# Turning the probabilities of block 2's 64-wide heads by VectorE blocks and a trip through memory instead of by TensorE

## What is computed

```python
def swa_gqa_sinks(q, k, v, sinks):
    ...
    scores = jnp.einsum("bnqhgd,bnkhd->bnhgqk", qb, kw).astype(jnp.float32) * (A_HEAD_DIM ** -0.5)
    ...
    scores = jnp.where(valid[None, :, None, None], scores, -jnp.inf)
    mx = jnp.maximum(jnp.max(scores, axis=-1, keepdims=True), sink)
    pr = jnp.exp(scores - mx)
    den = jnp.sum(pr, axis=-1, keepdims=True) + jnp.exp(sink - mx)
    attn = (pr / den).astype(v.dtype)
    out = jnp.einsum("bnhgqk,bnkhd->bnqhgd", attn, vw)
```

## Time and profile before

| | |
|---|---|
| median of 3 runs | 2307.66 us (2304.9 to 2308.04) |
| profiled execution, its own time | 2307.95 us |
| its span from first to last instruction | 2306.2 us |
| TensorE's mean granted clock | 0.998 of full speed |
| TensorE busy | 2283.7 us, 99% |
| VectorE busy | 1527.7 us, 66% |
| ScalarE busy | 1233.8 us, 53% |
| DMA engines, mean share | 61.7% by the weight and scratch queue |

### The profile page before, as it was taken

One profiled execution on the slowest core, in us unless ns is written; L12 is line 12 of the kernel. 1 busy time (PEld: TensorE's weight loads), 2 busy tenths in 40 slices (PEclk: granted clock), 3 DMA queues, 4 the chain that ended last, 5 costly groups with the idle time before them and its releaser, 6 DMA issues.

```text
span 2306.2 us, 30120 instructions
## 1 busy us (share of the span) xinstructions
PE 2283.7 (99%) x11144; PEld 1906.6 (83%) x11144; DVE 1527.7 (66%) x2411; ACT 1233.8 (53%) x1890; POOL 128.6 (6%) x141
## 2 busy tenths in 40 slices
PE   9999999999999999999999999999999999999999
PEld 8887888888878888888878888888888888888887
DVE  6656786566567866576587765664766587657654
ACT  6555544445555454354467654554554478555543
POOL 3140000004300000000000000000000000000000
PEclk9999999999999999999999999999999999999999
DMA  8556568756475587577564444875677564456772
GB/s 336 199 192 238 190 220 290 228 185 214 156 267 186 172 287 242 180 256 248 189 230 157 157 155 165 265 241 195 219 244 238 178 215 156 150 171 209 233 235 89
DMA packets 179857, 483.08 MB, mean 209 GB/s; under 512 B 20480, under 2 KB 65152, under 8 KB 178688
## 3 DMA queue, kind: packets, MB, share of 16 engines
q1 hardware_dynamic: 179712, 481.16, 61.7%
HBM read 452.24 MB, written 28.84 MB: 209 GB/s over the span
## 4 chain that ended last, share of the span: by engine, by line
PE 92%; DVE 3%; DMA 3%; ACT 1%; SPq 1%; issue 1%; POOL 0%; DVEq 0%; ACTq 0%
PE bank L2104 27%; PE bank L2109 27%; PE bank L2108 27%; PE bank L2151 2%; PE bank L2091 2%; PE bank L2092 2%; PE bank L2093 2%; DMA raw<-in_weights 1%; DVE wl L1593 1%; PE bank L2240 1%; SPq L1181 1%; DMA rg<-moved 1%; DMA moved<-rv 0%; PE bank L2202 0%; PE bank L2225 0%
## 5 line engine op out<-in xcount | busy, mean ns | idle before, releaser
L1363 ACT ACTIVATE wh<-raw 128x1024 fp32r<-128x1024 f32 (+1 forms) x778 | 814.5, 1051 | 768.1 <-PE bank L2109 690.8
L1593 DVE TENSOR_TENSOR wl<-raw,wh 128x1024 fp32r<-128x1024 f32 (+1 forms) x778 | 927.8, 1223 | 282.9 <-ACT wh L1363 279.3
L2104 PE MATMUL bank<-wh,xh 128*128 128x512 f32 (+1 forms) x2102 | 826.8, 393 | 5.0 <-issue 3.9
L2109 PE MATMUL bank<-wh,xl 128*128 128x512 f32 (+1 forms) x2102 | 816.8, 389 | 0.0
L2108 PE MATMUL bank<-wl,xh 128*128 128x512 f32 (+1 forms) x2102 | 815.7, 388 | 0.0
L2104 PEld LDWEIGHTS bank<-wh,xh 128*128 128x128 f32 x2102 | 395.2, 188 | 87.0 <-issue 7.3
L2109 PEld LDWEIGHTS bank<-wh,xl 128*128 128x128 f32 x2102 | 394.9, 188 | 81.0
L2108 PEld LDWEIGHTS bank<-wl,xh 128*128 128x128 f32 x2102 | 395.5, 188 | 76.9
L2104 PE MATMUL bank<-wh,act_h 128*128 128x512 f32 x528 | 206.0, 390 | 0.0
L2109 PE MATMUL bank<-wh,act_l 128*128 128x512 f32 x512 | 199.4, 389 | 0.0
L2108 PE MATMUL bank<-wl,act_h 128*128 128x512 f32 x512 | 199.3, 389 | 0.0
(11 more groups left out here) (347 smaller groups left out, 2066.9 us busy)
## 6 DMA issues: line engine op xcount, KB each, us to landing
raw<-in_weights SPq DMA_DIRECT2D x760, 512.0 KB, 4.3
turn<-ffn_s SPq DMA_DIRECT2D x264, 64.0 KB, 2.8
ffn_a<-turn SPq DMA_DIRECT2D x66, 256.0 KB, 4.7
raw<-in_weights SPq DMA_DIRECT2D x16, 384.0 KB, 3.2
ln<-in_ln SPq DMA_DIRECT2D x4, 1024.0 KB, 6.8
moved<-merged SPq DMA_DIRECT2D x32, 128.0 KB, 3.5
merged<-moved SPq DMA_DIRECT2D x8, 512.0 KB, 7.0
bias<-in_bias SPq DMA_DIRECT2D x2, 1024.0 KB, 9.3
```

Source lines behind the costliest of these rows:

```text
L1363: act.activation(wh[:, u % NH, 0:used(u)], raw[:, u % NR, 0:used(u)], ACT.Copy).then_inc(hi_done, 1)
L1593: dve.tensor_tensor(wl[:, u % NR, 0:used(u)], raw[:, u % NR, 0:used(u)], wh[:, u % NH, 0:used(u)].bitcast(F32), ALU.subtract).then_inc(lo_ ...
L2104: pe.matmul(out, h, w_h, start=st.first and i == 0, stop=False)
L2109: last = pe.matmul(out, lo, w_h, start=False, stop=ends)
```

## The change

1. Block 2's 16 heads: the 32 `probs_T` steps (16 in each layer) are gone. Instead each pair of heads has its probabilities, 128x768, transposed in 32x32 blocks by one VectorE instruction (`block`), written to scratch by four DMAs (`out`) and read back by one (`back`) into one of three buffers; `aa_pv` then reads them from there with a pattern of runs of 32 numbers. To make the order of the pieces fit, the two parts of a head's scores change places in `Pn`.
2. The pairs no longer go through `heads` but through a table: pair p starts at `PAIRS_AT[p]`, its `even` comes 2 later, `block` 3, `out` 4, `back` 6 and `aa_pv` 8 later. The digits of `weave` become lists of places (`PLACES_1`, `PLACES_2`).
3. The transfers of `ak`, `aq0` and `aq1` are issued earlier, among the units of the chunk `aq1` and after it, and the copies of `ak` and `aq0` stand at places 2 and 3 instead of 4 and 5.
4. In block 1 the steps from the copy of `rq` on stand earlier: the retention's steps at places 18 to 22 instead of 22 to 27, `block` of `rg0` and `rg1` at 23 instead of 28, their `out` at 24 and 25 instead of 29 and 30, `back` at 27 and 28 instead of 31 and 32, `halve` at 30 and 31 instead of 33 and 34. The loads `bm12` and `ln1` (1 MB each) stand at 31, behind these, instead of at 28, ahead of them. The later attention of block 1 stands one or two places earlier.

The places of block 2's pairs, worked out from the tables (scores / even / block / out / back / product):

| pair | before: scores, even, transposes, product | after: scores, even, block, out, back, product |
|---|---|---|
| 0 | 6, 7, 10 and 11, 12 | 6, 8, 9, 10, 12, 14 |
| 1 | 8, 12, 14 and 15, 16 | 8, 10, 11, 12, 14, 16 |
| 2 | 12, 16, 17 and 18, 19 | 12, 14, 15, 16, 18, 20 |
| 3 | 16, 18, 20 and 21, 23 | 15, 17, 18, 19, 21, 23 |
| 4 | 19, 22, 24 and 25, 27 | 19, 21, 22, 23, 25, 27 |
| 5 | 23, 26, 31 and 31, 32 | 22, 24, 25, 26, 28, 30 |
| 6 | 27, 32, 34 and 35, 37 | 26, 28, 29, 30, 32, 34 |
| 7 | 32, 36, 37 and 37, 38 | 29, 31, 32, 33, 35, 37 |

```diff
+PAIRS_AT = (6, 8, 12, 15, 19, 22, 26, 29)
+PAIR_STEPS = (("pv", 8), ("even", 2), ("s", 0), ("block", 3), ("out", 4), ("back", 6))
...
     for r in range(R):
         h_a = p.moved("block", f"rg{r}", rows=p.cc["rows"], dst="oa", tile=r)
-    p.add("load", name="bm12", s=ret_s3, roped=roped)
-    p.add("load", name="ln1", roped=roped)
     for r in range(R):
         h_a = p.moved("out", f"rg{r}", rows=p.cc["rows"], dst="oa", tile=r)
+    for r in range(R):
+        h_a = p.moved("back", f"rg{r}", rows=p.cc["rows"], dst="oa", tile=r)
     for src in ("dq", "dk"):
         c_d = p.moved("block", src, roped=q[src + "_rope"].n)
     for r in range(R):
-        h_a = p.moved("back", f"rg{r}", rows=p.cc["rows"], dst="oa", tile=r)
+        h_a = p.moved("halve", f"rg{r}", rows=p.cc["rows"], dst="oa", tile=r)
+    p.add("load", name="bm12", s=ret_s3, roped=roped)
+    p.add("load", name="ln1", roped=roped)
...
-    q["o"] = heads(p, "aa", AH // 2, scores, q["akv"])
+    done, evens = {}, {}
+    for _, _, what, pair in sorted((at + after, k, what, pair) for pair, at in enumerate(PAIRS_AT)
+                                   for k, (what, after) in enumerate(PAIR_STEPS)):
+        h = 2 * pair
+        if what == "s":
+            done[h] = scores(h)[1]
+        elif what == "even":
+            evens[pair] = p.count("even", 2)
+            p.add("even", h=h, of="aa", soft=done[h], m=p.count("shares"))
+        elif what == "block":
+            p.moved("block", f"pair{pair}", h=h, m=evens[pair])
+        elif what in ("out", "back"):
+            p.moved(what, f"pair{pair}", h=h)
+        else:
+            if h % 4 == 0:
+                q["o"] = p.next_o()
+            p.add("aa_pv", h=h, o=q["o"], name=f"pair{pair}", kept=q["akv"])
+            if h % 4 == 2:
+                p.add("o_split", h=h, o=q["o"], dst="ha", n=p.count("hi"), m=p.count("o_ready_0"))
...
+        flat = b["merged"][:, :, :].rearrange("p r n -> p (r n)")
+        for i in range(AH // 2):
+            stage[f"pair{i}"] = (flat[:, 0:768], flat[:, 768:1536], b["PT"][:, :, :].rearrange("p a n -> p (a n)"))[i % 3]
...
+                    elif k == "block" and st.name.startswith("pair"):
+                        dve.wait_ge(evened, st.m)
+                        dve.transpose(stage[st.name].rearrange("p (q m n) -> p q m n", q=4, m=6),
+                                      b["Pn"][:, st.h % 4:st.h % 4 + 2, :].rearrange("p a n -> p (a n)")
+                                      .rearrange("p (m q n) -> p q m n", m=6, q=4)).then_inc(blocked, 1)
...
-                        turned(st.t)
+                        if k == "ca_pv":
+                            turned(st.t)
+                        else:
+                            pe.wait_ge(moved_back[st.name], 16 * (st.l + 1))
...
+                        if k == "aa_pv":
+                            pairs = landed[st.name].rearrange("p (b m n) -> p m b n", b=4, m=6)
+                            sides = [(out, pairs[:, 3 * i:3 * i + 3], vs) for i, (out, pt, vs) in enumerate(sides)]
```

More of the change, by code:

```diff
@@ L168, in begin, with weave @@
         return kept
[L170 to L183, removed]
-        self.steps = before
[L185 to L191, removed]
+    def weave(self, before, dense, side, places):
+        assert len(places) == len(side), (len(places), len(side))
+        self.steps = before
+        left = sorted(zip(places, side), key=lambda pair: pair[0])
+        done = 0
+        for st in dense:
+            if st.kind == "unit":
+                while left and left[0][0] <= done:
+                    self.steps.append(left.pop(0)[1])
+                assert not any(sd.t is not None and sd.t == st.after_t for _, sd in left), st.u
+                assert not any(sd.kind == "o_split" and sd.o + 1 == st.after_o for _, sd in left), st.u
+                done += 1
+            self.steps.append(st)
+        self.steps += [sd for _, sd in left]
     def flip(self):
@@ L473, in plan_block1 @@
         merge(1, j, "w_branch_b", "ob", 4, j, ob_o + 1)
-    p.weave(before, dense_a + p.begin(), side, UNITS_AMONG_1)
+    p.weave(before, dense_a + p.begin(), side, PLACES_1)
     kept = p.begin()
@@ L655, in plan_block2, with out_early @@
     t_x = ffn("ffn1", 0, t_x, after_ffn1)
+    def out_early(i):
+        if i in OUT_EARLY:
+            p.moved("out", OUT_EARLY[i])
     def kept_rows(name, c0, dst, off, pair):
-        c = p.chunk(("w_in", [(c0, c0 + 512)]), "x", KT, 512, pair, t_x)
+        c = p.chunk(("w_in", [(c0, c0 + 512)]), "x", KT, 512, pair, t_x, among=out_early if name == "aq1" else None)
         q[name] = p.add("keep_kv" if name == "akv" else "keep", c=c, dst=dst, off=off)
@@ L677, in plan_block2 @@
             p.moved("block", name, kept=q[name])
+    p.moved("back", "ak")
     group = p.begin()
@@ L683, in plan_block2 @@
     p.add("m_narrow", c=c_log)
+    p.moved("back", "aq0")
+    p.moved("out", "aq1")
     p.add("p_split")
@@ L716, in plan_block2 @@
         p.add("a_sum", tile=r)
-    for what in ("out", "back", "copy"):
-        for name in ("ak", "aq0", "aq1"):
-            c_a = p.moved(what, name)
+    for name in ("ak", "aq0", "aq1"):
+        if name == "aq1":
+            p.moved("back", name)
+        c_a = p.moved("copy", name)
     p.add("m_log2")
@@ L751, in plan_block2 @@
     g_m = [gate2("hm", 5640, j, c_a[j]) for j in range(2)]
-    p.weave(before, dense_a + p.begin(), side, UNITS_AMONG_2)
+    p.weave(before, dense_a + p.begin(), side, PLACES_2)
     kept = p.begin()
@@ L906, in at @@
         return self.nc.alloc_sbuf_tensor_at(name, list(shape), dt, offset=self.base + offset), offset + size
-MOVED = ('rg0', 'rg1', 'oc', 'rq', 'rk', 'dq', 'dk', 'ak', 'aq0', 'aq1')
+MOVED = ("rg0", "rg1", "oc", "rq", "rk", "dq", "dk", "ak", "aq0", "aq1",
+         "pair0", "pair1", "pair2", "pair3", "pair4", "pair5", "pair6", "pair7")
 GAIN0 = {"gain_ffn1": 1, "gain_m": 2, "gain_ffn2": 3}
@@ L1184, in _ @@
                         sp.wait_ge(moved_out[st.name], 64 * (st.l + 1))
-                        sp.dma_start(landed[st.name], a["moved"][MOVED.index(st.name)].rearrange("(p n) -> p n", p=P))\
+                        part = landed[st.name]
+                        sp.dma_start(part, a["moved"][MOVED.index(st.name), 0:P * part.shape[1]].rearrange("(p n) -> p n", p=P))\
                           .then_inc(moved_back[st.name], 16)
@@ L1372, in _ @@
                             for r in (1, 0):
-                                part = b["Pn"][:, (st.h + i) % 4, 0:256] if r else b["Pn"][:, (st.h + i) % 4, 256:384]
+                                part = b["Pn"][:, (st.h + i) % 4, 128:384] if r else b["Pn"][:, (st.h + i) % 4, 0:128]
                                 at = 2 * (st.h % 8) + 2 * r + i
@@ L1546, in _ @@
                             for r in (1, 0):
-                                part = b["Pn"][:, n % 4, 0:256] if r else b["Pn"][:, n % 4, 256:384]
+                                part = b["Pn"][:, n % 4, 128:384] if r else b["Pn"][:, n % 4, 0:128]
                                 at = 16 * r + n
@@ L2238, in _ @@
                                   b["av"][:, :, st.h // 4 * ADH:(st.h // 4 + 1) * ADH]) for i in range(2)]
+                        if k == "aa_pv":
+                            pairs = landed[st.name].rearrange("p (b m n) -> p m b n", b=4, m=6)
+                            sides = [(out, pairs[:, 3 * i:3 * i + 3], vs) for i, (out, pt, vs) in enumerate(sides)]
+                        else:
+                            sides = [(out, pt.rearrange("p (m n) -> p m n", m=3), vs) for out, pt, vs in sides]
                         for out, pt, vs in sides:
-                            pe.matmul(out, vs[:, 0, :], pt[:, 0:S], start=True, stop=False)
+                            pe.matmul(out, vs[:, 0, :], pt[:, 0:2], start=True, stop=False)
                         for i, (out, pt, vs) in enumerate(sides):
-                            ins = pe.matmul(out[:, P:S], vs[:, 1, :], pt[:, S:384], start=False, stop=True)
+                            ins = pe.matmul(out[:, P:S], vs[:, 1, :], pt[:, 2], start=False, stop=True)
                             if st.h % 4:
```

25 lines of the change are left out of this document (15 added, 10 removed).

## The result

The changed kernel takes **2324.11 us** (median of 4 runs, 2321.93 to 2329.17) against 2306.28 for the kernel before on the same chip (2302.83 to 2308.04): a ratio of 1.0081, 95% interval 1.0065 to 1.0097. It is slower by 0.8%: 17.8 us by the medians, 18.7 by the ratio. The forecast was 2301.7 and its range ended at 2317. The profiled execution took 2329.17 us with a span of 2327.4. It is the longest of the four, 5 us above their median, so that what is read from its trace adds up to 21.2 us against the profiled execution before (2307.95), and not to 18.7.

What follows compares the result with a forecast made beforehand. TensorE, busy 99% of the span, was taken to bound the kernel. From 2307.95 us, 24.0 taken away and 18.0 added gave 2301.95, or 2301.7 us allowing for the profiled execution lying 0.29 above the median; range 2288 to 2317.

Steps and rivals of the forecast that it cites:

- (1): Block 1's merge: an earlier read-back removes TensorE's wait in both layers, 11.7 us gained, 8.2 idle and 3.5 slow clock.
- (2): Block 2's first scores in layer 2: the 1.4 us wait goes, since the copy of aq0 comes two places earlier.
- (3): Block 2's 32 TensorE transposes of probabilities, 0.34 us each, go: 10.9 us gained, all on TensorE's queue.
- (6): Block 2's products: TensorE newly waits for read-backs, 9 us in each layer, 18 in all, walked at pairs 0 and 6.
- (4): Block 2: 16 VectorE transposes of 128x768 are added, 0.95 us each, 7.6 us in each layer.
- (5): Block 2's transfers per pair: writes 2.9 us, read-back 5.2, at least 9.5 us from block's end to landing.
- (7): Block 2's products: reading runs of 32 numbers costs TensorE nothing extra; bounds were nothing or 12.8 us.
- (8): SyncE's queue is held up waiting for a late block, up to 5 us; 13 raw buffers cover that.
- Rival C: Block 2's weave: VectorE becomes the bound, late blocks delaying masks, exponentials and roundings; 2317.7 us, chance 0.20, milder form 0.04.
- The rule: Block 2's transposes: by the skill's page the change puts work where it is dearer; TensorE's 10.9 us would stay.

Runs made afterwards that it cites:

- e2: The kernel before with only block 1's new order and places, block 2 untouched: 2296.06 us, 0.9958; run again 2298.52 us, 0.9963.
- e7: e2 plus early transfers of ak, aq0 and aq1, and load ln1 moved behind the read-backs of dq and dk: 2293.45 us, 0.9958; again 2295.08 us, 0.9950.
- e9: e8 plus 16 VectorE transposes of 128x768 into a buffer nobody reads, at the second transposes' places: 2297.08 us, 0.9963 of the kernel before.
- e1: The changed kernel with the load of gain_ffn2 moved behind pair 7's read-back: 2314.25 us, 1.0035 of the kernel before.
- e8: e2 without block 2's 32 TensorE transposes of probabilities and ScalarE's 32 copies, nothing in their place: 2287.62 us, 0.9921 of the kernel before.
- e3: The changed kernel without block 2's writes and read-backs, products reading VectorE's blocks in place: 2299.48 us, 0.9967 of the kernel before.
- e6: The changed kernel with pairs 3.6 units apart, products 9 units behind scores, gain_ffn2's load behind pair 7's read-back: 2307.30 us, 1.0011 of the kernel before.

## Why the prediction was wrong, point by point

**(1) Block 1's merge: right in the mechanism, a little dear.** The wait for `oa_l` is gone, as the earlier trace rows and the 4.35 us said it would be. Forecast 11.7; block 1's part alone gives 11.1 and 11.4 by the traces, 9.7 and 8.5 by the ratios. That the traces come so near is partly luck. The two merges themselves gave 5.3 us each, 10.6. What was priced at nothing, "late next", was not nothing: the wait for `dk` took 2.3 us of it back in e2 and 5.5 in the profiled execution of the change. Some 3 us came from places further on, of which the prediction has no word. The writes of `dq` and `dk` behind the two 1 MB loads took 10.6 us to land (165 to 200 us of the trace), against 4.6 before, and the copy came 2.4 and 1.2 us late in this execution. In e7, with one of the two loads behind them, they took 8.9 us, and the wait was gone.

**(2) Scores of layer 2: right.** 1.5 us by the table above, for 1.4.

**(3) Transposes, 10.9 us: right as a term, wrong in the sum.** Alone it is worth 8.5 to 10.3. It was added to the others as if they were independent. It takes from VectorE the time in which it caught up, and with the blocks in place it is worth nothing: e9 stands where e2 stands. Point (6) did say "in a stretch that the missing transposes shorten by 4.8", and then walked only two pairs.

**(4), (5) Block and transfers: right or too dear.** 0.97 us for 0.95; writes 2.2 for 2.9; read-back 4.3 for 5.2. The exception is the 6.7 of e1. The page "DMA: Bandwidth & Descriptors", section "Anatomy of one DMA", of the Trainium skill would give 2.9 us by estimate. It states its two figures for transfers that GpSimd issues, which the prediction left out; for these, which SyncE issues, the trace has 4.3.

**(6) The wait for the read-back: this is the step that failed.** Forecast were 18 us, as waits alone. The waits for read-backs are 25.8, and with the slow clock and the bank waits that come with them the term is 39.6 (18.9 and 20.7). The walk left out one transfer in SyncE's queue, took VectorE's delay too small, and the likeliest value left out the slow clock. Pair 0 was walked well: 3.2 us forecast, 2.0 measured, with the read-back issued behind pair 1's writes as described. Block 1's gain brings every time forward by 7.0, so the forecast issue at 1234.1 becomes 1227.1; it was 1227.29. At pair 6 the walk put the block's end at 1302.1, or 1295.1; it was 1297.77, 2.7 later, where I had taken 2.5 off for VectorE's idle time. From the block's end to the issue of the read-back I took 1.4 and 2.9 us; it was 9.8, **5.5 more**, all of it the load of `gain_ffn2`. The read-back itself was 1.1 shorter. So the loss up to there was 9.4 + 2.7 + 5.5 - 1.1 = 16.5 us, and 2.6 of slow clock behind it, which the likeliest value left out, make 19.1; the matmuls give 18.9.

The load could have been seen. At pair 0 I followed SyncE's queue step by step, and at pair 6 counted only the transfers of the pairs. The trace before showed the load issued at 1302.12, between two weight loads 4.6 us apart where 2.7 is usual.

**(7) The strided product: right.** Nothing was forecast. From 1289.76 to the next unit at 1290.57 in the trace after are 0.81 us, 0.80 before.

**(8) SyncE held up: wrong in kind.** Weight loads were covered, as said. Behind the held queue stood the read-back.

**Rival C** came nearest, 2317.7 by "VectorE becomes the bound of the weave" at a chance of 0.20. Its mechanism, late steps of VectorE and ScalarE that hold up TensorE, is shown by e8 and e9 and by the bank waits of e3 and e6, though not by the number it was argued from: VectorE was 76% busy in this stretch and not 88%. It is not the whole: without the trips' length and the load it would have ended at about the time of block 1's part alone. What I held against it, that every wait of TensorE lets VectorE catch up, is so behind pair 6's wait, where VectorE is busy 0.34 of 5.3 us. It fits the waits coming at single places and not at every pair. **The rule** that a 128x128 transpose belongs on TensorE ("VectorE: DVE Perf Modes", "Rules for kernel authors", the Trainium skill) speaks for the kernel before. The runs agree for the whole change. Before any trip, the 9.7 us of blocks and the 8.5 of transposes are equal within their error (9.9 and 10.3 by the traces); the trip's 15.7 us decide.

## What to carry to other kernels

Two gains that draw on the same slack don't add up: taking work from the bounding engine and giving work to the one behind it are one edit. Its price is the lag of the second engine, to be read from where it trails now (masks behind the scores: 3.5 us before and 5.0 after at place 19, 3.8 and 9.2 at pair 6) and from how much of its idle time is waiting for a third. Before a transfer gets a deadline in an in-order queue, list everything that stands ahead of it there and what each waits for; a load that is late today without harm is the first suspect. And try the parts of a bundled change apart: here its small reorderings were worth 0.5%, and its main part cost more than twice that (from e7 to the change, 0.0123).

## What the runs showed of the hardware

A read-back of 384 KB took 4.3 us (median of 12 in the change). With two 512 KB loads issued within 1.5 us ahead of it, it took 4.9 to 6.7 in e1. Writes of 128 KB behind two 1 MB loads took 10.6 us to land, behind one 8.9 (e7), and 4.6 before the change. SyncE's queue is in order for its waits too: a load that waited for VectorE until 1307.20 held back a read-back whose writes had been issued by 1299.57. A read by TensorE in runs of 32 numbers cost no more than a contiguous one (0.81 against 0.80 us a product). Behind the wait of 9.95 us the granted clock was 0.51 for 5.3 us, and it was 0.75 on the average of the wait itself, so the lower clock had begun before work came back.
